# Expert layers on one Trainium2 core: 0/1 matrix per pair, spread in two-part results, eight weight slots filled from the norm on, embedding inputs loaded at the end

## The reference, cut to what matters

```python
def expert_choice_moe(h, w_router, w_gate_e, w_up_e, w_down_e):
    cap = EC_CAPACITY * s // N_EXPERTS                       # 64 tokens per expert
    affinity = softmax((h @ w_router), axis=-1)              # 512 x 16
    top_aff, idx = lax.top_k(swapaxes(affinity, 1, 2), cap)  # each expert chooses 64 tokens
    xe = h[bidx, idx]
    hid = silu(xe @ w_gate_e) * (xe @ w_up_e)
    ye = hid @ w_down_e
    return zeros_like(h).at[bidx, idx].add(ye * top_aff[..., None])

x = x + expert_choice_moe(rms_norm(x, g_moe[i]), w_router[i], w_exp_gate[i], w_exp_up[i], w_exp_down[i])
ple_gate = sigmoid(rms_norm(x, g_ple[i]) @ w_ple_gate[i])
x = x + ple_gate * (p[i] @ w_ple[i])
```

## Time and profile before

| | us |
|---|---|
| median of three runs | 4260.84 |
| lowest and highest run | 4259.82, 4261.68 |
| the profiled execution, its own time | 4260.53 |
| its span from first to last instruction | 4258.8 |
| PE matmul busy | 3643.9 (86%) |
| PE weight load busy | 2415.4 (57%) |
| DVE busy | 1711.8 (40%) |
| ACT busy | 1048.9 (25%) |
| mean granted clock of PE | 0.934 of full speed |

### The profile page before, as it was taken

How to read it: one execution, slowest core, us unless ns; L and a number is a source line. 1 busy time by engine, 2 the same in 40 slices (tenths; PEclk the granted TensorE clock), 3 DMA queues, 4 the chain that set the end, 5 groups by cost and what they waited for, 6 DMA issues and landing times. The chain is left out here.

```text
span 4258.8 us, 45164 instructions
## 1 busy us (share of the span) xinstructions
PE 3643.9 (86%) x17408; PEld 2415.4 (57%) x17408; DVE 1711.8 (40%) x2996; ACT 1048.9 (25%) x1623; POOL 24.6 (1%) x34
## 2 busy tenths in 40 slices
PE   7669996999987769986999885998899969998998
PEld 5546674434445646665444443765666746666666
DVE  2475643111132475743111133236744322476433
ACT  2233321000022233321000022333332124333321
POOL 0010000000000010000000000000000000000000
PEclk9879997999998879997999997999999989999999
DMA  4021124999943121123999954111122241111222
GB/s 150 28 87 51 62 87 185 408 416 408 409 162 113 37 87 50 54 91 151 410 413 408 409 200 178 60 40 45 55 80 75 89 189 50 48 47 56 74 75 99
DMA packets 133511, 653.03 MB, mean 153 GB/s; under 512 B 20836, under 2 KB 43364, under 8 KB 67032
## 3 DMA queue, kind: packets, MB, share of 16 engines
q1 hardware_dynamic: 128088, 642.17, 39.1%
q10 hardware_dynamic: 5248, 8.52, 0.6%
HBM read 640.00 MB, written 14.84 MB: 154 GB/s over the span
## 5 line engine op out<-in xcount | busy, mean ns | idle before, releaser
L1430 PE MATMUL ps<-normed_T_hi,ring_split 128*128 128x512 f32 (+1 forms) x1952 | 639.1, 409 | 40.9 <-PEq L268 14.6
L1430 PEld LDWEIGHTS ps<-normed_T_hi,ring_split 128*128 128x128 f32 (+1 forms) x1952 | 370.5, 193 | 154.6 <-issue 44.8
L1430 PE MATMUL ps<-normed_T_lo,ring_split 128*128 128x512 f32 (+1 forms) x976 | 388.8, 398 | 0.0
L2079 PE MATMUL ps<-normed_T_hi,ring_split 128*128 128x512 f32 x1024 | 339.4, 413 | 18.5 <-DVE branches L2338 16.5
L1706 DVE TENSOR_TENSOR ring_split<-weight_ring,ring_split 128x2048 fp32r<-128x2048 f32 x76 | 174.0, 2290 | 301.4 <-ACT ring_split L1591 301.3
L1027 PE MATMUL ps<-weight_ring,projected 128*64 128x512 f32 x1280 | 281.0, 593 | 15.4 <-DVE projected L1072 15.4
L2079 PEld LDWEIGHTS ps<-normed_T_hi,ring_split 128*128 128x128 f32 x1024 | 194.9, 194 | 90.6 <-issue 29.7
L257 PE MATMUL ps<-weights_hi,normed_T_hi 128*128 128x472 f32 (+1 forms) x512 | 199.4, 389 | 44.8 <-DVE weights_lo L369 34.5
L1430 PEld LDWEIGHTS ps<-normed_T_lo,ring_split 128*128 128x128 f32 (+1 forms) x976 | 187.5, 192 | 42.5
L1090 DVE TENSOR_TENSOR residual<-residual,ps 128x512 f32<-128x512 f32 x128 | 88.0, 688 | 290.9 <-PE ps L1048 290.9
L2079 PE MATMUL ps<-normed_T_lo,ring_split 128*128 128x512 f32 x512 | 204.0, 398 | 0.0
(11 more groups left out here) (391 smaller groups left out, 5792.2 us busy)
## 6 DMA issues: line engine op xcount, KB each, us to landing
weight_ring<-in_w_exp_gate SPq DMA_DIRECT2D x96, 1024.0 KB, 18.9
weight_ring<-in_w_slabs SPq DMA_DIRECT2D x78, 1024.0 KB, 4.9
spare_weights<-in_w_exp_up SPq DMA_DIRECT2D x64, 1024.0 KB, 24.6
weight_ring<-in_w_exp_up SPq DMA_DIRECT2D x64, 1024.0 KB, 11.1
spare_weights<-in_w_exp_down SPq DMA_DIRECT2D x64, 1024.0 KB, 17.1
weight_ring<-in_w_branch_gate SPq DMA_DIRECT2D x32, 1024.0 KB, 5.0
weight_ring<-in_w_exp_down SPq DMA_DIRECT2D x32, 1024.0 KB, 13.4
weight_ring<-in_w_ada SPq DMA_DIRECT2D x16, 1536.0 KB, 12.7
```

The costliest lines, as they stand in the source:

```text
L1430: ins = e.matmul(dst, lhs(k, m), rhs(k, m), start=k == 0 and m == 0, stop=k == KD - 1 and m == 2)
L2079: ins = e.matmul(dst, lhs(k, m), rhs(k, m), start=k == 0 and m == 0, stop=k == KD - 1 and m == 2)
```

## The change

- Second norm: SP loads the router's weights there and asks for the first six weight slots. Route: SP asks for slots 6 and 7 when the router's products are done. There are now eight slots, three in `weight_ring`, one and a half in `branches`, one and a half in `projected`, two in `spare_weights`.
- Route: nothing is stored to DRAM. The 0/1 matrix is built for one pair only (`choose`), and for the next pair inside the expert stage.
- Experts: `spread` is the 0/1 matrix turned by PE and copied by ACT. The weight of each slot comes from four matmuls of the 0/1 matrix with two columns of the affinities; it is applied when the result is taken, in a high part (ACT) and a low part (DVE), both float32r. PE multiplies `spread` by both. The gather for the next pair stands between down and spread. PE's list is a loop of two pairs that runs three times, and two pairs behind it.
- Experts, end: SP asks for the embedding's first inputs, whose semaphores are those of the slots. The last norm loads its gain alone, and splits the first gate weights ahead of the turned rows on ACT.
- First norm: the four bias spreads stand at the end of `project_stage`'s SP list.

```diff
 def norm_stage(...):
                     signals.zero_other(e)
-                    if ple is not None:
-                        e.dma_start(p_T, a["p"][ple, :, :, :]).then_inc(s["side_landed"], 16)
-                        e.dma_start(ple_side[:, :, :], ple_side_w(ple, 0)).then_inc(s["side_landed"], 16)
-                        for kh in range(2):
-                            land(e, s, kh, a["w_ple_gate"][ple, kh * 512:(kh + 1) * 512, 0:512], 512)
...
                     for dst, src in loads:
                         e.dma_start(dst, src).then_inc(s["inputs_loaded"], 16)
+                    if experts_of is not None:
+                        for v in range(6):
+                            load_expert_weights(e, experts_of, 0, v)
                     if loads:
                         e.wait_ge(s["inputs_loaded"], 16 * len(loads))
-                    if spread_bias:
-                        for h in range(4):
-                            e.dma_start(skew[...], bias_rows[h, :].partition_broadcast(P)).then_inc(s["side_landed"], 16)
-                        e.wait_ge(s["side_landed"], 64)
...
+                    if ple is not None:
+                        e.wait_ge(slot_loaded[0], EXPERT_LOADS + 16)
+                        e.activation(W_hi[:, 0, :], landing[:, 0, :], ACT.Copy).then_inc(s["slab_hi"], 1)
                     if bias_col is None:
                         scaled_hi(e, s, KD, scale_col)
...
+        def choose(e, i):
+            return e.tensor_tensor(chosen.rearrange("p t (x c) -> p t x c", x=2), iota.unsqueeze(1).unsqueeze(1).to_broadcast([P, NT, 2, CAP]),
+                                   ranks_tok[:, :, bass.ds(i * 2, 2)].unsqueeze(3).to_broadcast([P, NT, 2, CAP]), ALU.is_equal)
 def route_stage(l):
-                    e.dma_start(wr, a["w_router"][l, :, :].rearrange("(k p) n -> p k n", p=P)).then_inc(s["inputs_loaded"], 16)
-                    for v in range(4):
-                        load_expert_weights(e, l, 0, v)
-                    e.wait_ge(s["stage_a"], 1)
-                    for v in range(4, 6):
+                    e.wait_ge(s["product_ready"], 1)
+                    for v in range(6, 8):
                         load_expert_weights(e, l, 0, v)
...
 def expert_stage(l, gain_col):   # SP
+                    for u in range(8, 24):
+                        e.wait_ge(s["weights_free"], u - 7)
+                        load_expert_weights(e, l, 0, u)
+                    with e.Fori(1, n_pairs // 2) as i2:
+                        for u in range(24):
+                            e.wait_ge(s["weights_free"], i2 * 24 + (u - 7))
+                            load_expert_weights(e, l, i2, u)
+                    for kh in range(2):
+                        e.wait_ge(s["weights_free"], 12 * n_pairs - (7 - kh))
+                        e.dma_start(landing[:, kh, :]..., a["w_ple_gate"][l, kh * 512:(kh + 1) * 512, 0:512]...).then_inc(slot_loaded[kh], 16)
+                    e.wait_ge(s["weights_free"], 12 * n_pairs - 5)
+                    e.dma_start(p_T, a["p"][l, :, :, :]).then_inc(slot_loaded[2], 16)
+                    e.dma_start(ple_side[:, :, :], ple_side_w(l, 0)).then_inc(slot_loaded[2], 16)
...
                 # PE, one pair
+                        for t in range(NT):
+                            e.transpose(PS[:, 4, t * P:(t + 1) * P], chosen[:, t, :], ident)
+                        for t in range(NT):
+                            ins = e.matmul(PS[:, 5, 0:2], chosen[:, t, :], affinity[:, t, bass.ds(i * 2, 2)], start=t == 0, stop=t == NT - 1)
+                        ins.then_inc(s["rotated"], 1)
                         e.wait_ge(s["stage_b"], i * 2 + 2)
-                        e.wait_ge(s["stage_h"], i * 8 + 8)
                         for v in range(8):
+                            if v % 2 == 0:
+                                e.wait_ge(s["stage_h"], i * 8 + (5 + v // 2))
                             products(v)
...
                         for v in range(8, 12):
                             products(v)
+                        if not last:
+                            e.wait_ge(s["hi_ready"], i + 1)
+                            gather(i + 1)
+                        e.wait_ge(s["lo_ready"], i + 1)
                         for q in range(8):
                             t, half = q // 2, q % 2
                             if q >= 4:
                                 e.wait_ge(s["stage_h"], i * 8 + (q + 5))
-                            e.matmul(PS[:, q % 4, :], spread[...], ye[...], start=True, stop=True)
+                            for part in (result_hi, result_lo):
+                                ins = e.matmul(PS[:, q % 4, :], spread[...], part[:, half, :], start=part is result_hi, stop=part is result_lo)
...
+                    with e.Fori(0, n_pairs // 2 - 1) as i2:
+                        pair(i2, 0, False)
+                        pair(i2, 1, False)
+                    pair(n_pairs // 2 - 1, 0, False)
+                    pair(n_pairs // 2 - 1, 1, True)
...
                 # ACT
+                        e.activation(spread[:, :], PS[:, 4, :], ACT.Copy).then_inc(s["output_ready"], 1)
+                        e.activation(result_hi[:, :, :], PS[:, 4:6, :], ACT.Copy, scale=slot_weight).then_inc(s["output_taken"], 1)
-                        for ex in range(2):
-                            for dst, which in ((who, 0), (weight, 1)):
-                                e.dma_start(dst[...], route[...].to_broadcast([64, S])).then_inc(s["inputs_loaded"], 16)
                 # DVE
+                            ins = e.tensor_copy(slot_weight[64 * ex:64 * ex + 64, :], PS[64 * ex:64 * ex + 64, 5, ex:ex + 1])
+                            choose(e, i + 1).then_inc(s["hi_ready"], 1)
+                        e.scalar_tensor_tensor(result_lo[:, :, :], PS[:, 4:6, :], slot_weight, result_hi[:, :, :].bitcast(F32), ALU.mult, ALU.subtract).then_inc(s["lo_ready"], 1)
+                            take_gathered(i + 1)
-                        e.scalar_tensor_tensor(spread, who, slot_of, weight, ALU.is_equal, ALU.mult).then_inc(s["output_ready"], 1)
```

More of the change, by code:

```diff
@@ L99, in mixer_kernel @@
         signals = Signals(nc, ctx)
-        slot_loaded = [ctx.enter_context(nc.semaphore(f"expert_slot_loaded_{n}")) for n in range(6)]
+        slot_loaded = [ctx.enter_context(nc.semaphore(f"expert_slot_loaded_{n}")) for n in range(8)]
         X = sb("residual", [P, NT, D])
@@ L155, in mixer_kernel @@
         gate_saved = nc.dram_tensor("gate_scratch", (1, D), F32, kind="Internal").ap()
-        route = nc.dram_tensor("route_scratch", (2, N_EXP, S), F32, kind="Internal").ap()
         def z_view(width):
@@ L404, in _ @@
                     load(pairs - 1, 1, final=True)
+                    for h in range(4):
+                        e.dma_start(skew[h:h + 1, :].rearrange("a (p c) -> (a p) c", p=P)[:, 0:1024], bias_rows[h, :].partition_broadcast(P)).then_inc(s["side_landed"], 16)
+                    e.wait_ge(s["side_landed"], 64)
                 @block.tensor
@@ L862, in _ @@
                     e.wait_ge(s[st.name], st.value)
-        chosen = Zr[:, 4096:8192].rearrange("p (t n) -> p t n", t=NT)
-        halves = [W[:, 2048 * n:2048 * (n + 1)] for n in range(6)] + [T[:, 4096:6144], Zr[:, 9216:11264]] + [spare[:, 2048 * n:2048 * (n + 1)] for n in range(4)]
-        ring = [[halves[2 * n + ex].rearrange("p (k n) -> p k n", k=4) for ex in range(2)] for n in range(6)]
+        chosen = T[:, 3072:3584].rearrange("p (t n) -> p t n", t=NT)
+        affinity = small[:, 192:256].rearrange("p (t n) -> p t n", t=NT)
@@ new lines, in mixer_kernel @@
+        ranks_tok = small[:, 256:320].rearrange("p (t n) -> p t n", t=NT)
+        slot_weight = small[:, 320:321]
+        router_w = T[:, 4096:4224].rearrange("p (k n) -> p k n", k=KD)
+        halves = [W[:, 2048 * n:2048 * (n + 1)] for n in range(6)] + [R[:, 2048 * n:2048 * (n + 1)] for n in range(3)]
+        halves += [Zr[:, 2048 * n:2048 * (n + 1)] for n in range(2, 5)] + [spare[:, 2048 * n:2048 * (n + 1)] for n in range(4)]
+        ring = [[halves[2 * n + ex].rearrange("p (k n) -> p k n", k=4) for ex in range(2)] for n in range(8)]
@@ L975, in _ @@
                     e.wait_ge(s[st.name], st.value)
-                    for t in range(NT):
-                        e.tensor_tensor(chosen[:, t, :].rearrange("p (x c) -> p x c", x=N_EXP), iota.unsqueeze(1).to_broadcast([P, N_EXP, CAP]),
-                                           ranks_tok[:, t, :].unsqueeze(2).to_broadcast([P, N_EXP, CAP]), ALU.is_equal).then_inc(s["vector_step"], st.add("vector_step"))
+                    choose(e, 0).then_inc(s["vector_step"], st.add("vector_step"))
                     e.wait_ge(s[st.name], st.value)
@@ L987, in expert_stage @@
             s = signals.stage()
-            xe = Zr[:, 8192:9216].rearrange("p (k n) -> p k n", k=KD)
-            who = R[:, 0:512]
-            weight = R[:, 512:1024]
-            spread = R[:, 1024:1536]
```

(11 more changed lines are left out.)

97 lines of the change are left out of this document (44 added, 53 removed).

## The result

The changed kernel takes 4162.0 us (median of four runs, 4161.74 to 4167.18) against 4260.97 us for the kernel before on the same chip: a ratio of 0.977, interval 0.9754 to 0.9788. The forecast was 4160, range 4140 to 4188. The profiled execution took 4161.74 us with a span of 4160.0, against 4260.53 and 4258.8 before: 98.8 us of span to be found.

What follows compares the result with a forecast made beforehand. PE and DMA were both taken as nearly full in the expert stage. Savings of 11.6 + 2 x (7.2 + 30.3 + 7.3) = 101.2 us from 4260.5 gave 4159.3, forecast as 4160 us, range 4140 to 4188.

Steps and rivals of the forecast that it cites:

- The two lines: Expert stage: PE at 57.6 us a pair, DMA at 59.6; over the stage 453.1 and 452.1 us, taken to coincide.
- The two joints that no row showed: Pair on PE: spread in 4.3 us instead of 6.86, and added transposes and small weight matmuls 1.6 us.
- The three other terms of the pair: Pair on PE: gate and up with the hid chain 30.92 us, down 13.72, gather 7.1.
- the PE line of the stage: Expert stage on PE: seven pairs at 57.6 us, plus 44.9 and the tail's 8.8, less 3.8: 453.1 us.
- First norm: Bias spreads moved away, next stage starts 0.5 us after the arithmetic: saves 4.9 and 6.7, together 11.6 us.
- Route: Second norm and route: router load saves 3.2 us, smaller 0/1 build 4.0; 7.2 a layer, 6.6 before SP's first late issue.
- Last norm: Embedding inputs arrive early and the weight split moves ahead of the turned copies: saves 7.3 us a layer.
- the two expert stages: Expert stage, one per layer: falls from 483.9 to 453 us, saving 30.9, or 30.3 after the first pair's 0.6.
- (a): Rival: PE binds longer, gather hides less or spread and small matmuls cost more; 4209 us, halfway 4184; chance 0.14.
- (b): Rival: shorter PE pauses also remove two clock ramps of 2.7 us a layer; 4149 us; chance 0.15.
- (c): Rival: PE must refetch the longer two-pair loop's instructions through full DMA engines; 4462 us, slower than before; chance 0.04.
- (d): Rival: last two weight slots not full before the first product; stage 462 us, time 4178; chance 0.02.

## Why the prediction was right, and where it was off

The two lines carry the result, and each was seen alone. PE: 57.6 us a pair forecast, 57.4 measured in four of seven intervals. DMA: 59.6 forecast, 59.3 to 59.5 measured in the kernels where it binds. Eight slots and no broadcasts are what keeps DMA under PE (experiments with six slots and with broadcasts). The two joints that no row showed came out at 3.99 (forecast 4.3) for the spread and 1.32 (forecast 1.6) for turns and weights; the gather covered both copies in full. The three other terms of the pair came out longer, 31.09, 13.89 and 7.16 for 30.92, 13.72 and 7.1, so that misses in both directions nearly cancel in the 57.4. (The 13.72 stands in no row; the earlier trace rows has 14.00.)

**The term that failed** is the PE line of the stage, "7 x 57.6 + 44.9 + 8.8 - 3.8". It took every pair at full clock. In three pairs the two pauses of the earlier trace rows (1.32 and 0.83 there) are followed by a spell at half clock that costs 1.4 to 1.8 us, 4.8 in all; 453 + 4.8 is 457.8, and 457.5 was measured. Filling the pauses with empty work took the spells away and gave 453.7. The kernel before had such a spell too, in one pair of layer 1 and in two of layer 2, here beside a pair that has none:

```profile
757.00:759.00 2.00, 2.00 (x8) 0.72 (x6) 0.00 (x0) 0.00 (x0) 0.00 (x0) 0.50 0.99 414
941.00:945.00 4.00, 3.85 (x18) 1.61 (x20) 0.10 (x2) 0.00 (x0) 0.00 (x0) 1.00 1.01 422
2044.00:2046.00 2.00, 2.00 (x6) 0.60 (x4) 0.00 (x0) 0.00 (x0) 0.00 (x0) 0.50 1.02 426
2477.00:2479.00 2.00, 2.00 (x6) 0.60 (x4) 0.00 (x0) 0.00 (x0) 0.00 (x0) 0.50 1.00 418
```

A look at those pairs would have put the term into the sum, though not that it grows from one pair of layer 1 to three.

Other sizes. First norm: 10.5 instead of 11.6. The next stage starts 0.84 us after the arithmetic (20.95 + 5.68 to 27.47, and as much in layer 2) where 0.5 was forecast, and layer 2's arithmetic itself took 0.4 longer than before. Route: 6.8 and 6.0 for 6.6; SP's twelve issues in the norm ended at 665.5, and the norm's arithmetic only at 670.0, so they were hidden as forecast. That the slots are asked for so early is worth nothing by itself, which the prediction had not separated; what gains in this step is the router's load (DVE waits 0.32 us instead of 3.56) and the 0/1 matrix for one pair (0.69 instead of 4.63). Last norm: 8.0 and 6.9 for 7.3. So the sum: 101.2, less 6.7 for the two expert stages, 1.1 for the first norms and 0.4 for the routes, 0.3 more for the last norms, and 5.5 gained in stages that the change leaves alone, makes the 98.8 of the spans. Those 5.5 are not owed to the change as far as the runs show: the same stages in the traces of the two later runs of the changed kernel, against the same trace before, gain 1.2 and 3.8. Without the 5.5 the time would have been 4167, which is also what the first of these runs took. So the range held on the strength of the two lines, but that the sum came within 2 us of the result is in part luck: 6.7 us that the two expert stages fell short stood against 5.5 that no part of the change accounts for.

The rivals. (a), PE slower than summed by its joints: the joints cost less than forecast; what slowed PE was the clock, and the time stayed near the forecast. (b), ramps given back: the embedding products run at 7.11 / 16 = 0.44 a pass instead of 0.60, which the forecast had in it, but more than that did not come; in the expert stage ramps were added instead. (c), code loading: it did not come. The instruction queue q8 carried 124 packets in the whole kernel instead of 110. In layer 1's expert stage five of them moved between 710 and 820 us, the first passage of the loop of two pairs, none between 820 and 1065, its second and third passage, and four from 1065 on, with the two pairs that stand behind it. Pairs behind a turn of the loop are no longer than the others. The Trainium skill, Runtime: NRT & Kernel Launch, section "Instruction fetch mechanics", gives PE room for 2048 instructions; some 1200 that repeat without a fetch agree with this, and not with that section's sentence on two blocks. (d), slots not full: they were asked for at 678.43 at the latest, and PE waited for no weights in the whole stage.

On the DMA ceiling, the trace stays at 424 GB/s at share 1.01 with one queue of 1 MB transfers, and the kernels bound by DMA go by that number. The Trainium skill, DMA: Bandwidth & Descriptors, section "Where 436 GB/s comes from", gives 435 for the ports into SBUF and about 358 as what binds between HBM and SBUF. The traces decide, and on one core they agree with neither: 423 to 424 held through both expert stages is above the second, and no expert stage here reached the first.

Left open: why three pairs of eight have the spell and the rest not, with the same pauses. Experiments moved it (four, six or all of eight, and none), but no run varied the pause alone in steps. Left open too is how much of the route's 6.8 and 6.0 us goes to the router's load and how much to the 0/1 matrix: no run took back one alone.

## What to carry to other kernels

Draw one line per resource through a repeated stage, prefilled buffers included, and price every edit on the longer line: here the spread or the place of the gather, taken back alone, cost nearly the whole of the stage's 26 us, and the broadcasts, put back, cost 17 of them. When PE is the longer line and pauses for a microsecond or two in each turn, look at the granted clock right behind the pause in every repeat, not in one, and put useful work of the next turn there. Loads asked for earlier than the longest cover that they already have buy nothing.

## What was unexpected of the hardware

Behind a pause of 1.32 us and one of 0.98 us, 1.1 us of passes apart, in an engine that is otherwise busy all the time, the granted clock falls from 2.4 to 1.2 GHz, in three, four, six or eight of eight pairs depending on what else the pair does; it costs 1.4 to 1.8 us each time, and it stays away when the pauses are filled. Nineteen passes of 128 columns a pair whose results nobody reads took 8.5 us off a 4165 us kernel. Four broadcasts a pair, 0.52 MB together, beside a full queue lower the total rate from 424 to 412 GB/s over whole pairs.
